# A decoder layer's expert rounds: waits for landed weights against constants, one step per round, in place of counts read from a table

## The reference

```python
D_MODEL, N_EGROUPS, EXP_PER_GROUP, N_EXPERTS, TOP_K, D_FF_E = 1024, 4, 4, 16, 2, 256

def hier_moe(h, w_router_g, w_router_e, w_gate, w_up, w_down):
    p_grp = softmax(h @ w_router_g)                 # 4 groups, the best one is taken
    g_hot = one_hot(argmax(p_grp))
    le_sel = (logits of the 4 experts of that group)
    top_v, top_i = lax.top_k(softmax(le_sel), TOP_K)   # its best 2 experts
    comb = one_hot(e_idx) * (top_v / sum(top_v)) * p_top
    act = silu(h @ w_gate[e]) * (h @ w_up[e]) * comb[e]
    return sum over e of act @ w_down[e]
```

## Time and profile before

| | us |
|---|---|
| median of 3 runs (lowest to highest) | 1797.66 (1796.91 to 1800.92) |
| the profiled execution, own time | 1796.45 |
| its span, first to last instruction | 1794.8 |
| expert phase in it, first e_win copy to last silu | 1380.6 to 1717.4 |

### The profile page before, as it was taken

One profiled execution on the slowest core, in us unless ns is written; L12 is line 12 of the kernel. 1 busy time (PEld: TensorE's weight loads), 2 busy tenths in 40 slices (PEclk: granted clock), 3 DMA queues, 4 the chain that ended last, 5 costly groups with the idle time before them and its releaser, 6 DMA issues. The chain is left out here.

```text
span 1794.8 us, 24645 instructions
## 1 busy us (share of the span) xinstructions
PE 1456.7 (81%) x8651; PEld 1292.8 (72%) x8651; DVE 990.0 (55%) x1295; ACT 624.7 (35%) x951; POOL 227.4 (13%) x294
## 2 busy tenths in 40 slices
PE   3689999999997368788787792899973899899940
PEld 2689999999996167777776671688853687788830
DVE  4775554311321456666665434544425798799927
ACT  3322223111011222232232102333322687788823
POOL 0000001000000032422431000000000111111122
PEclk8899999999998779899898555899985999999975
DMA  3111122332112431121120214533223877774238
GB/s 123 55 35 47 47 72 85 103 96 62 58 61 77 143 60 26 26 49 28 26 41 22 103 47 160 164 106 106 83 85 141 326 279 285 259 257 178 83 141 321
DMA packets 91579, 200.52 MB, mean 112 GB/s; under 512 B 39227, under 2 KB 59963, under 8 KB 86655
## 3 DMA queue, kind: packets, MB, share of 16 engines
q1 hardware_dynamic: 74031, 135.48, 23.6%
q0 software_dynamic: 17488, 64.32, 9.4%
HBM read 205.96 MB, written 47.29 MB: 141 GB/s over the span
## 5 line engine op out<-in xcount | busy, mean ns | idle before, releaser
L87 DVE TENSOR_TENSOR c_wlo<-c_w,c_whi 128x1024 fp32r<-128x1024 f32 x40 | 49.0, 1225 | 262.7 <-ACT c_whi L82 262.3
L98 PE MATMUL c_ps<-hn_lo,c_whi 128*128 128x368 f32 x960 | 182.4, 332 | 7.0 <-DVE c_wlo L87 7.0
L98 PE MATMUL c_ps<-hn_hi,c_wlo 128*128 128x368 f32 x960 | 181.3, 331 | 0.0
L98 PE MATMUL c_ps<-hn_hi,c_whi 128*128 128x368 f32 x960 | 181.1, 331 | 0.0
L98 PEld LDWEIGHTS c_ps<-hn_lo,c_whi 128*128 128x128 f32 x960 | 164.9, 189 | 7.3 <-DVE c_wlo L87 7.3
L2237 DVE TENSOR_TENSOR e_winlo<-e_win,e_winhi 128x2048 fp32r<-128x2048 f32 x66 | 151.1, 2292 | 30.8 <-ACT e_winhi L2185 29.2
L98 PEld LDWEIGHTS c_ps<-hn_hi,c_wlo 128*128 128x128 f32 x960 | 164.3, 188 | 0.0
L98 PEld LDWEIGHTS c_ps<-hn_hi,c_whi 128*128 128x128 f32 x960 | 163.9, 188 | 0.0
L2185 ACT CAST e_winhi<-e_win 128x2048 fp32r x66 | 123.0, 1917 | 51.7 <-issue 34.5
L82 ACT CAST c_whi<-c_w 128x1024 fp32r<-128x1024 f32 x40 | 42.1, 1052 | 224.7 <-PE c_ps L98 219.2
L510 DVE SCALAR_TENSOR_TENSOR c_y<-c_raw,c_taps,c_y 128x1128 f32<-128x1128 f32 x60 | 83.6, 1394 | 8.7 <-DVE c_y L506 0.2
(11 more groups left out here) (464 smaller groups left out, 2855.6 us busy)
## 6 DMA issues: line engine op xcount, KB each, us to landing
e_win<-in_w_gate_up SPq DMA_DIRECT2D x33, 2048.0 KB
e_wdn<-in_w_down SPq DMA_DIRECT2D x33, 1024.0 KB
c_w<-in_w_in SPq DMA_DIRECT2D x40, 512.0 KB, 3.6
expert_rows<-e_ys POOLq DMA_DIRECT2D x33, 512.0 KB, 3.0
rc_eb<-g_rows SPq DMA_DIRECT2D x10, 624.0 KB, 5.4
o_land<-in_w_out SPq DMA_DIRECT2D x8, 768.0 KB, 4.9
rc_gb<-g_rows SPq DMA_DIRECT2D x11, 507.0 KB
n_x<-in_xT SPq DMA_DIRECT2D x2, 2208.0 KB, 10.1
```

The source lines that it names most:

```text
L87: return dve.tensor_tensor(dst, src, hi.bitcast(F32), ALU.subtract)
L98: mm = pe.matmul(dst, left(x, k), right(z, k), start=(n == 0 and k == 0), stop=(n == 2 and k == ks - 1))
```

## The change

`split_win` and `split_wdn` on ACT no longer read T_NEED; in round r they wait for 16 x (r + 1), the count that stands when the loads issued (or passed over) by SP's iteration r-1 have landed. T_HERE is read once a round on ACT and once on DVE, and the register is kept for the later uses. SP, PE and POOL have the same instructions in the same order as before, but for line numbers.

```diff
         @block.scalar
         def _(act):
+            slots = {}
+
             def split_win(r):
-                here = act.value_load(tab[0:1, T_HERE, r:r + 1], min_val=0, max_val=1)
-                need = act.value_load(tab[0:1, T_NEED, r:r + 1], min_val=16, max_val=16 * (R + 1))
-                act.wait_ge(ex.win_loaded, need)
+                here = slots[r] = act.value_load(tab[0:1, T_HERE, r:r + 1], min_val=0, max_val=1)
+                act.wait_ge(ex.win_loaded, 16 * (r + 1))
                 if r >= 2:
                     act.wait_ge(gate_up, r - 1)
...
             def split_wdn(r):
-                here = act.value_load(tab[0:1, T_HERE, r:r + 1], min_val=0, max_val=1)
-                need = act.value_load(tab[0:1, T_NEED, r:r + 1], min_val=16, max_val=16 * (R + 1))
-                act.wait_ge(ex.wdn_loaded, need)
+                here = slots.pop(r)
+                act.wait_ge(ex.wdn_loaded, 16 * (r + 1))
...
         @block.vector
         def _(dve):
+            slots = {}
+
             def split_win(r, g):
-                here = dve.value_load(tab[0:1, T_HERE, r:r + 1], min_val=0, max_val=1)
+                if g == 0:
+                    slots[r] = dve.value_load(tab[0:1, T_HERE, r:r + 1], min_val=0, max_val=1)
+                here = slots[r]
...
                 if r < R:
-                    here = dve.value_load(tab[0:1, T_HERE, r:r + 1], min_val=0, max_val=1)
+                    here = slots.pop(r)
                     dve.wait_ge(wdn_hi, r + 1)
```

## The result

The change makes the kernel slower: 1814.96 us median of five runs (1814.47 to 1816.91) against 1796.91 of five runs before (1795.07 to 1800.92), ratio 1.0098, 95% interval 1.0085 to 1.0111. The profiled execution took 1816.55 us with a span of 1814.9, which is 20.1 more than the 1794.8 before. The direction and the mechanism were forecast, the size was not: 1825.5 was predicted, and the range ended at 1816.0.

The account below looks back on a forecast made before the run. PE and the short way silu, gated, transpose were taken to make the round. Stalls of 29.7 us less 1.1 for table reads, 28.6 on 1796.45, gave 1825.0, median 1826.3; the forecast said 1825.5, range 1816 to 1835.

Parts of the forecast that it names:

- rounds 8, 18, 22 over 9.57: Rounds following an undisturbed one: ACT's e_win wait makes them 13.51 us long, +3.94 each.
- slow rounds 5, 9, 19, 23: Rounds behind long rounds 4, 8, 18 and 22: PE's clock falls, 11.40 us, +1.83 each.
- round 4: Its e_win load, issued behind a real e_wdn load, makes the round 13.81 us, +4.24.
- rounds 6, 10, 20: Rounds following a slow one: the load is issued earlier, so the round is 11.51 us, +1.94 each.
- start, to the silu of round 3: The first e_win copy on ACT has one table read less ahead of it: -0.4 us.
- end, behind the last silu: PE waits for the last e_wdn part, which comes 0.76 us earlier: -0.7 us.
- full stall: ACT's e_win wait behind an undisturbed round: 13.51 us, +3.94, and +1.83 in the next round, together 5.77.
- rival 1: Counts of passed-over loads land late, so rounds 24 to 31 wait too: 16 us, 1842, chance 0.07.
- rival 2: Every new e_win wait on ACT costs a full stall: 39.8 us, 1837, chance 0.05.
- The table reads: Three fewer reads a round on ACT, hidden by PE; they count only at start and end, together -1.1 us.
- When it lands: e_win load, issue to ACT's copy: 8.81 and 9.71 us, mean 9.26; 10.57 behind a real e_wdn load.
- the prediction's own check: Issue, load and copy-to-silu times added, 0.48 + 9.26 + 3.60 = 13.34 us, set against rounds 12 and 15.

Follow-up runs that it names:

- wait alone: The kernel before, with both of ACT's weight waits on the constant 16 x (r + 1) and every table read left in: 1824.02 us, ratio 1.0154.
- second profile of the change: The changed kernel measured once more, word for word: 1815.67 us, ratio 1.0116, span 1811.8.
- ACT's reads back: The changed kernel with ACT's table reads as before, four a round, T_NEED read and not used: 1820.56 us, ratio 1.0141.
- SP's reads out of the way: The changed kernel with SP's three table reads for the next iteration made before its e_wdn issue, while it waits for DVE: 1798.05 us, ratio 1.0008.
- the filler work: The changed kernel with 20 more unused transposes on PE in the gaps of eleven rounds: 1815.59 us, ratio 1.0113.

## Why the prediction was wrong in size

Point by point, in the profiled executions, where 20.1 us stand against the predicted 28.6:

| term of the sum | predicted | measured |
|---|---|---|
| rounds 8, 18, 22 over 9.57 | +11.8 | 13.01, 12.50, 12.01: +8.8 |
| slow rounds 5, 9, 19, 23 | +7.3 | 11.44, 11.40, 11.29, 11.42: +7.3 |
| round 4 | +4.2 | 11.84: +2.3 |
| rounds 6, 10, 20 | +5.8 | 10.61, 11.42, 10.92: +4.2 |
| rounds 7, 11, 21 | 0 | 9.80, 9.79, 9.80: +0.7 |
| rounds 12 to 17 | +0.5 | -0.4 |
| start, to the silu of round 3 | -0.4 | -1.3 |
| rounds 24 to 32 | 0 | 0.0 |
| end, behind the last silu | -0.7 | -1.5 |

The places were right, and the pattern of full stall, slow round, half stall, quiet round is in the windows above. That passed-over loads count up in time (rival 1 said not) is shown by rounds 24 to 31 at 9.6 us, and the full stalls all the way (rival 2) did not come, for the reason given against it.

By whole kernels, the miss of 10.5 us has two parts. The wait alone was put at 29.7 us and measured 27.1 (2.6 too much). The reads were put at 1.1 us, and beside the stalls they are worth 9 (8 too little).

The step that failed is therefore *The table reads*, with "What hides it is PE". It was argued from an undisturbed round, where it holds: alone the reads gave about 1.7 us, not clear of zero. But the same text puts the price of a stall as the time of issue plus the time of the load, and in a stalled round PE hides nothing; there SP's issue leads, and both engines' reads delay it. Against the kernel with the wait alone, the change issues a load 0.5 us earlier in a round behind one of 9.8 us (9.62 to 9.66 us behind the silu two rounds before, in rounds 8, 18 and 22; that kernel has 10.16 to 10.18, in rounds 6, 10 and 22), and 0.25 us earlier in a round behind a slow one (10.20 to 10.24 in rounds 6, 10 and 20, against 10.44 to 10.48 in rounds 8 and 20). From the first silu to the last, the wait alone has 352.3 us, the changed kernel 346.3 and 345.6 in its two profiles, and the kernel before 324.2: 6 to 7 us for the reads inside the rounds, where the prediction counted nothing. The rest of the 9 us can't be placed from single executions. In particular the start and the end, where it counted its 1.1 us, do not show the reads: the wait-alone kernel, with all of them in, has its first silu at 1392.84 us and 75.6 us behind its last one, the changed kernel 1392.63 and 76.0. This is the interaction: the same edit holds the cost and a part of the remedy.

The second term that was mis-sized is the time of a load, *When it lands*. The sum has 9.26 us for six of the seven new stalls and 10.57 for round 4, whose load also came behind a real e_wdn load, as that of round 3 did. From issue to copy the seven measured 8.20 to 9.57, with a mean of 8.77; the means in the second profile of the change and in the wait-alone kernel are 8.76 and 8.78. For round 4 it is 8.59, and 9.77 in the second profile. In the profile above this term makes 4.8 of the 6.5 us by which the seven stalls fell short. The issue makes 1.3: it was kept at 10.05 us behind the silu two rounds before, so it came 0.6 us earlier than taken in rounds 8, 18 and 22 (-0.16, -0.13 and -0.18 in place of +0.48), as taken in round 4, and 0.15 to 0.26 later in rounds 6, 10 and 20. The last 0.5 is the 13.51 us taken for a full stall, where the prediction's own check gives 13.34. That the wait alone still came near its 29.7 us is partly luck: its loads were shorter than taken, and its issues behind slow rounds later.

The rows before the change had two loads behind an e_wdn load that moved nothing, and one behind a real one. That was too few for a price that moves by 1 to 2 us between executions. What makes that time 8 to 11 us is not settled: half a megabyte more per round changed its mean by 0.1 us. The Trainium skill, DMA: Bandwidth & Descriptors, Anatomy of one DMA, from which the prediction takes its estimate of 6.8 us, gives that fit for DMAs on GpSimd's path. These loads go out on SP's queue, and 6.8 us is too short for every load that ACT waited for in the changed kernel (7.96 to 11.19).

## What to carry to other kernels

A wait on a plain count asks for everything issued so far; where loads run ahead of use, it can ask for a transfer that only just left, so compare for each wait the time of that issue with the time of the wait. Cost the parts of an edit in the stage that the other parts create, not in the one that was profiled: work that was covered before can be uncovered by the edit itself. And when a load is late, look first at what the issuing queue does before it; here two moves in SP's program took 37 us off the changed kernel, 17 by making three table reads while SP waits and 20 by putting one issue in front of another, and left it 19 below the kernel before.

## What was not expected of the hardware

The time that SP takes to read one integer of a small table from SBUF depends on what other engines do: a median of 268 to 273 ns, 534 to 541 in the four kernels in which ACT has its two reads in front of the e_wdn copy, and 818 when POOL issued twice as many product writes. In the kernel before, ACT's own reads have medians of 273 to 278 ns. The cause was not found; in the quiet round shown above the reads of ACT and SP do not overlap in time. With three of them between two DMA issues of one queue the issues are 2.2 to 2.7 us apart, and 0.53 with the reads made earlier.

How long a gap on PE is does not tell here whether the clock falls behind it. In the changed kernel, PE stands idle for 2.13 us in front of L2145 at 1507.64 and for 2.55 us at 1439.97. Behind the first the granted clock stayed at 1.00 (round 11, 9.79 us), behind the second it fell (round 5, 0.85). In the second profile a gap of 2.50 us, in round 6, was followed by 1.00 (round 7 above). Two gaps of other kernels lie further out, one with ACT's reads back and one with SP's reads out of the way:

```profile
1463.36 0.44 PE L2145 MATMUL e_psa<-masks,e_gated 128*128 128x128 f32 x2 [1.89 <-DVE e_gated L2260]
...
1569.33 0.44 PE L2156 MATMUL e_psa<-masks,e_gated 128*128 128x128 f32 x2 [3.33 <-DVE e_gated L2271]
```

Behind the gap of 1.89 us the clock fell (0.58 over 1464.20 to 1467.60), and behind the one of 3.33 it stayed at 1.00 over the 9.77 us that follow. In both cases PE had run 1.0 us of transposes ahead of the gap, at full clock. The kernel's time hardly depends on it, as the filler work showed.
